# Last mixer: one product per head and level for both token tiles, a turned square at the end, and the exponent differences on GpSimd

## The chip, the cores and the metric

The kernel runs on one core of a Trainium2 chip. The time is device microseconds of that core, as the median of several runs; a profiled execution is one further run, in which every instruction's start and end were recorded. Its engines are called PE (TensorE, with PEld for its weight loads), DVE (VectorE), ACT (ScalarE), POOL (GpSimd) and SP (SyncE, which here issues the weight loads).

## What is computed

The reference is a chain of eight stages over 256 tokens of width 1024: a SwiGLU layer, an attention and gated linear attention mixer, a second SwiGLU layer, an embedding gate, a second mixer, a convolutional feed-forward layer, the HGRN2 mixer, and a last feed-forward layer. The change touches the HGRN2 mixer, the stage "hg". Cut to what matters:

```python
def hgrn2_chunkwise(q, k, v, log_f):
    # S_t = diag(f_t) S_{t-1} + k_t v_t^T with k_t = 1 - f_t, o_t = S_t^T q_t
    diff = G_[..., :, None, :] - G_[..., None, :, :]      # G: running sum of log_f
    pair_decay = jnp.exp(jnp.where(incl, diff, -jnp.inf))
    attn = jnp.einsum("bhld,bhlsd,bhsd->bhls", q_, pair_decay, k_)
    ...
def hgrn2_mixer(u, w_in, lower_bound, norm_gain, w_out):
    q, f, i, gate = jnp.split(u @ w_in, ...)
    log_f = jnp.logaddexp(jnp.log(lb), jnp.log1p(-lb) + jax.nn.log_sigmoid(ff))
    k = (1.0 - lb) * jax.nn.sigmoid(-ff)
    o = hgrn2_chunkwise(silu(q), k, i, log_f)             # 8 heads of 128
    y = head_rms_norm(o, norm_gain) * jax.nn.silu(gate)
    return y.astype(u.dtype) @ w_out
```

For every head the weight of key token j in query token i is the sum over 128 channels of q[i] * exp(G[i] - G[j]) * k[j], for j up to i.

## The kernel before

**Levels.** The kernel doesn't form the decay of each pair. It splits the triangle j < i into levels: at level `half` (128, 64, ..., 1: `ALL_LEVELS`, numbered n = 0 to 7) the tokens are cut in blocks of 2 x half, and the pairs with j in the left and i in the right half of one block are handled. With the value of G at the block's middle as a reference, the exponents G[i] - ref and ref - G[j] are computed apart (`dve_level_x`, two subtractions of 512 columns, lines 1695 and 1697), made into exponentials by ACT (`act_level`, line 1714), and multiplied into the queries and the keys by DVE (`dve_level_l`, lines 1707 and 1709). The result, `h_l[n % 2]`, has decayed keys in left and decayed queries in right places, 4 heads x 256 tokens wide. PE multiplies it with itself (`pe_h_level`, line 2394 by `per_tile`): one 128 x 128 product for each head and each of the two tiles of 128 tokens, 8 for a level, into one of two pairs of PSUM banks. DVE puts the part that belongs to the level into the square of attention weights, `h_at[u]`, by a copy under a mask (`dve_h_put`, line 2981; the masks are the constants `level64` to `level1`). Level 0 (half = 128) joins the two tiles, has 4 products (line 2956) and its own place `h_cross`; number 8 is the diagonal. All of these products are fp32, and an fp32 product of PE stands in the trace as two instructions.

**Units and steps.** The 8 heads are two units u of 4 heads. `H_STEPS` is the list of 18 steps g, nine for each unit in the order 8, 0, 1, ..., 7. m = 0 to 15 counts levels without the diagonal. Behind each step's products PE multiplies one or two half-slots ("pieces") of the projection weights (`pieces_after(g)`), which supply the forget gate, query, output gate and value of the units. Each fp32 weight piece is split into a high part by ACT (`split_hi`, line 298) and a low part by DVE (`split_lo`, line 303), each 1024 columns; PE multiplies three times with them (lines 329 to 331).

**Order.** The order on each engine is the order of the code, and every engine works through its queue strictly, waiting where an instruction waits. DVE's turn for one level m is: put of two steps back, the two products of level m, at times a scan of G for unit 1 (line 2900), the two differences of level m + 2, the low half of a weight piece. ACT's turn is: the high half of a piece, the exponential of level m + 2, and in some turns a block of its own: `act_h_forget(1)` at m = 2 (two sigmoids, a table load before and behind, four logarithms), `act_h_q(1)` at m = 5, the gates at m = 7 and 13. POOL in this stage has only two clearings of `h_at`.

**The end of the stage.** When a unit's squares are complete PE multiplies them with the values (`pe_h_out`, lines 3008 and 3010). ACT squares the output, DVE applies the gain and sums the squares, ACT takes the root, DVE gates (line 3044), PE turns the rows (line 337), ACT and DVE split them into high and low, and PE multiplies them with the output weights, pieces 0 to 7 of "hgo". For unit 1 the order on PE is: piece 0, output products of unit 1, pieces 1 and 2, turns of unit 1's rows, pieces 3 to 7.

Of the kernel before, what the change touches and what calls it, by code (L numbers as in the profile page):

```python
# [8 lines left out]
U32 = mybir.dt.uint32  # L9
# [30 lines left out]
def shape_constants():  # L40
# [11 lines left out]
    for name, f in (("cos", np.cos), ("sin", np.sin), ("nsin", lambda a: -np.sin(a))):  # L52
        for t in range(NT):
            parts[f"{name}{t}"] = f(ang[t].astype(np.float64))
    at, cols, n = {}, [], 0
    for name, a in parts.items():
        at[name] = n
        n += a.shape[1]
        cols.append(a.astype(np.float32))
# [30 lines left out]
def build(nc, A, out, numbered, stop=None):  # L90
# [3 lines left out]
    with ctx:  # L94
# [19 lines left out]
        const = sb("const", [P, A["const"].shape[1]])  # L114
# [57 lines left out]
        out_sem = sem("stored")  # L172

# [1514 lines left out]
        def dve_level_x(dve, X, n, half, b, e, ready):  # L1688
# [3 lines left out]
            for name in ready:  # L1692
                dve.wait_ge(*after(name))
            ref = blocks(b)[:, :, half - 1:half].broadcast_to([P, b.shape[1] // (2 * half), half])
            nc.vector.tensor_tensor(blocks(e)[:, :, right], blocks(b)[:, :, right], ref, ALU.subtract)\
                .then_inc(*steps.did("dve", f"{X}.x{n}r"))
            nc.vector.tensor_tensor(blocks(e)[:, :, left], ref, blocks(b)[:, :, left], ALU.subtract)\
                .then_inc(*steps.did("dve", f"{X}.x{n}"))
# [80 lines left out]
        def dve_g_exponents(dve, n):  # L1779

            dve_level_x(dve, "g", n, ALL_LEVELS[n], gb, g_e[n % 2], [f"g.l{n - 2}"] if n >= 2 else ["g.b"])
# [5 lines left out]
        def dve_g_levels(dve):  # L1787

            levels = len(ALL_LEVELS)
            for n in range(2, levels):  # L1790
                dve_g_put(dve, n - 1)
                dve_g_decayed(dve, n)
                if n + 2 < levels:
                    dve_g_exponents(dve, n + 2)
# [144 lines left out]
        def dve_mix0(dve):  # L1939
# [24 lines left out]
            dve_g_exponents(dve, 0)  # L1964
            dve_a_den(dve)
            dve_g_exponents(dve, 1)
# [3 lines left out]
            for n in range(2):  # L1970
                dve_g_decayed(dve, n)
                dve_g_exponents(dve, n + 2)
# [860 lines left out]
        h_sil = (arena[:, 10752:11776], hk[0])  # L2833
        h_sq = (hk[0], arena[:, 6144:7168])
# [103 lines left out]
        def pe_h_level(pe, g):  # L2938
# [15 lines left out]
            if n == 0:  # L2954
# [6 lines left out]
        def dve_h_put(dve, g):  # L2961
# [9 lines left out]
            before = {8: f"{X}.at0", 1: f"{X}.put8"}.get(n, f"{X}.put{n - 1}")  # L2971
            dve.wait_ge(*after(before))
            half = ALL_LEVELS[n] if n < len(ALL_LEVELS) else 0
            if half:
                right = lambda a: a.rearrange("p (k m r) -> p k m r", k=8, r=2 * half)[:, :, :, half:]
                mask = cst(f"level{half}").rearrange("p (m r) -> p m r", r=2 * half)[:, :, half:]
                mask = mask.bitcast(U32).unsqueeze(1).broadcast_to([P, 8, P // (2 * half), half])
            else:
# [404 lines left out]
```

## Time and profile before

| | us |
|---|---|
| median of 3 runs | 1234.22 |
| lowest, highest | 1234.01, 1234.27 |
| span of the profiled execution | 1232.7 |
| PE busy | 1215.1 |
| DVE busy | 847.2 |
| ACT busy | 682.4 |
| POOL busy | 53.0 |

The span is from the first to the last instruction; the median stands 1.5 us above it. The stage hg lies at about 885 to 1037 us. In a row of the order of time the time of an instruction runs from its start to its end; on a busy queue the next one starts a little before the end, so that the distance of the starts is the smaller number. "Idle before" is the time that the engine stood in front of it, with what ended it. The durations of PE's products overlap, and a sum of them says nothing; the union of their spans does.

### The profile page before, as it was taken

To read this page: it belongs to the slowest core of one execution; us is meant where nothing else is said; L and a number is where in the kernel's file an instruction comes from. 1 tells how busy PE (TensorE), PEld (TensorE's weight loads), DVE (VectorE), ACT (ScalarE), POOL (GpSimd) and SP (SyncE) were. 2 spreads that over 40 slices of the span, in tenths; PEclk is the share of its full clock that TensorE was granted. 3 is DMA by queue.
4 is the path that set the end of the run, shared out by engine and by line. 5 is a ranking of instruction groups with operands and counts; after the bars stand their busy time and mean duration, and the time that the engine had idled before them with its cause. 6 is when DMAs were issued, how large, how long until landed. Compare 5 with 4: busy or idle time off the path is not lost. (4 is left out here: it accounts for less than half of the span.)

```text
span 1232.7 us, 19105 instructions
## 1 busy us (share of the span) xinstructions
PE 1215.1 (99%) x7351; PEld 1069.0 (87%) x7351; DVE 847.2 (69%) x1153; ACT 682.4 (55%) x1009; POOL 53.0 (4%) x84
## 2 busy tenths in 40 slices
PE   8999999999999999999999999999999999999998
PEld 6888888887888888889898799999899887999997
DVE  5555457778654446757966776776868988766666
ACT  5444446464544435656635765555775657655455
POOL 0400000010000000101400000000000000000000
PEclk9999999999999999999999999999999999999999
DMA  9965555425645555544322665555553335555620
GB/s 336 272 221 175 174 205 175 138 69 171 212 173 174 183 204 205 174 157 138 134 69 87 205 205 192 176 172 177 204 205 100 107 100 209 178 185 184 204 103 35
DMA packets 139206, 209.10 MB, mean 170 GB/s; under 512 B 9949, under 2 KB 101235, under 8 KB 139137
## 3 DMA queue, kind: packets, MB, share of 16 engines
q1 hardware_dynamic: 136256, 199.39, 48.1%
q0 software_dynamic: 2864, 8.76, 2.5%
q8 instruction: 46, 0.75, 0.3%
q14 instruction: 24, 0.19, 0.0%
q10 hardware_dynamic: 16, 0.00, 0.0%
HBM read 207.08 MB, written 1.05 MB: 169 GB/s over the span
## 5 line engine op out<-in xcount | busy, mean ns | idle before, releaser
L303 DVE TENSOR_TENSOR wlo<-raw,whi 128x1024 fp32r<-128x1024 f32 x374 | 440.6, 1221 | 45.1 <-ACT whi L298 43.3
L298 ACT ACTIVATE whi<-raw 128x1024 fp32r<-128x1024 f32 x374 | 374.1, 1050 | 42.4 <-PE psum L331 40.4
L329 PE MATMUL psum<-whi,xh 128*128 128x512 f32 (+1 forms) x688 | 275.3, 400 | 4.8 <-DVE wlo L303 3.5
L331 PE MATMUL psum<-whi,xl 128*128 128x512 f32 (+1 forms) x688 | 267.4, 389 | 0.0
L330 PE MATMUL psum<-wlo,xh 128*128 128x512 f32 (+1 forms) x688 | 266.8, 388 | 0.0
L329 PE MATMUL psum<-xh,whi 128*128 128x256 f32 x928 | 263.5, 284 | 0.0
L330 PE MATMUL psum<-xl,whi 128*128 128x256 f32 x928 | 262.6, 283 | 0.0
L331 PE MATMUL psum<-xh,wlo 128*128 128x256 f32 x928 | 262.6, 283 | 0.0
L329 PEld LDWEIGHTS psum<-xh,whi 128*128 128x128 f32 x928 | 177.9, 192 | 0.9
L330 PEld LDWEIGHTS psum<-xl,whi 128*128 128x128 f32 x928 | 178.0, 192 | 0.7
L331 PEld LDWEIGHTS psum<-xh,wlo 128*128 128x128 f32 x928 | 178.0, 192 | 0.0
L329 PEld LDWEIGHTS psum<-whi,xh 128*128 128x128 f32 x688 | 129.6, 188 | 36.2 <-DVE wlo L303 4.2
L331 PEld LDWEIGHTS psum<-whi,xl 128*128 128x128 f32 x688 | 129.5, 188 | 27.5
L330 PEld LDWEIGHTS psum<-wlo,xh 128*128 128x128 f32 x688 | 129.8, 189 | 23.6
L329 PE MATMUL psum<-whi,hidh 128*128 128x512 f32 x352 | 137.5, 391 | 0.0
L330 PE MATMUL psum<-wlo,hidh 128*128 128x512 f32 x352 | 137.2, 390 | 0.0
L331 PE MATMUL psum<-whi,hidl 128*128 128x512 f32 x352 | 137.0, 389 | 0.0
L1175 DVE SCALAR_TENSOR_TENSOR arena<-psum,taps,arena 128x254 f32<-128x254 f32 (+1 forms) x176 | 74.8, 477 | 82.3 <-ACT arena L1141 78.1
L1195 DVE TENSOR_TENSOR hidl<-psum,hidh 128x512 fp32r<-128x512 f32 x22 | 15.2, 692 | 149.0 <-ACT hidh L1191 149.0
L1191 ACT ACTIVATE hidh<-psum 128x512 fp32r<-128x512 f32 x22 | 13.2, 598 | 166.0 <-PE psum L1076 166.0
L1141 ACT ACTIVATE arena<-psum,taps 128x256 f32<-128x256 f32 x88 | 42.4, 563 | 90.6 <-PE psum L331 79.8
L331 PEld LDWEIGHTS psum<-whi,hidl 128*128 128x128 f32 x352 | 66.1, 188 | 13.9
(373 smaller groups left out, 1184.5 us busy)
## 6 DMA issues: line engine op xcount, KB each, us to landing
raw<-in_ffn_w_up SPq DMA_DIRECT2D x131, 512.0 KB, 5.2
raw<-in_ffn_w_down SPq DMA_DIRECT2D x88, 512.0 KB, 4.4
raw<-in_ffn_w_gate SPq DMA_DIRECT2D x43, 512.0 KB, 4.6
raw<-in_c_w_in SPq DMA_DIRECT2D x32, 512.0 KB, 4.7
raw<-in_ab_w_in SPq DMA_DIRECT2D x28, 512.0 KB, 4.7
raw<-in_w_in SPq DMA_DIRECT2D x18, 512.0 KB, 4.5
raw<-in_w_out SPq DMA_DIRECT2D x8, 512.0 KB, 4.1
raw<-in_ple_w_gate SPq DMA_DIRECT2D x8, 512.0 KB, 5.0
```

Of the source, the lines that this page charges most:

```text
L298: nc.scalar.activation(hi, r, ACT.Copy).then_inc(hi_done, 1)
L303: nc.vector.tensor_tensor(lo, r, hi.bitcast(F32), ALU.subtract).then_inc(lo_done, 1)
L329: nc.tensor.matmul(pe_out, sh, mh, start=start, stop=False, skip_group_check=True)
L330: nc.tensor.matmul(pe_out, sh, ml, start=False, stop=False, skip_group_check=True)
L331: return nc.tensor.matmul(pe_out, sl, mh, start=False, stop=stop, skip_group_check=True)
L1141: last = nc.scalar.activation(cg[:, q, j, c, :], gate_or_up(n, q, j, c), ACT.Identity, scale=tap(n, 2, f), bias=tap(n, 3, f))
L1175: last = nc.vector.scalar_tensor_tensor(y, gate_or_up(n, q, j, c)[:, 0:SEQ - lag], tap(n, k, g * 2 + (FC * j + c)), y, ALU.mult, ALU.add)
L1191: nc.scalar.activation(hidh[:, q], hidden_columns(q) if n < 2 else hp[:, q], ACT.Copy).then_inc(hid_hi, 1)
L1195: nc.vector.tensor_tensor(hidl[:, q], hidden_columns(q) if n < 2 else hp[:, q], hidh[:, q].bitcast(F32), ALU.subtract)\
```

## The change

**One product for both tiles.** In levels 1 to 7 DVE now writes the decayed queries of tile 0 into the right places of tile 1 and the other way round (two products of 256 columns in place of one of 512; the keys as before). PE then multiplies, for each head, tile 0's part of `h_l` with tile 1's: left places of tile 0 are tile 0's keys and meet tile 0's queries, above the diagonal; right places of tile 0 are tile 1's queries and meet tile 1's keys, below the diagonal. So there are 4 products in place of 8 at these levels, and one square holds both tiles.

**Gathering.** The square of a unit is `h_both[u]`, 4 heads x 128. Level 1 is copied whole by ACT, level 2 by ACT in its two diagonal quarters (`act_h_put`, at m % 8 = 3 and 4), levels 3 to 7 by DVE under the masks `block32` to `block2`, new constants, 4 heads x 128 columns. `h_both[0]` lies where the masks `level64` to `level8` were; the new masks come by a DMA of POOL in the stage ffn2. Then DVE copies the upper triangle into tile 0 of `h_at[u]`, PE turns the square (4 transposes of 128 x 128, `pe_h_turn`), and DVE copies the upper triangle of the turned one into tile 1 (`dve_h_upper`).

**Order.** Unit 0's turn is behind step 9 and its output products move from step 9 to step 10. In the tail PE's order becomes: piece 0, turn of unit 1's square, piece 1, output products of unit 1, piece 2, turns of unit 1's rows, piece 3. On DVE both copies of unit 1's upper triangle stand ahead of the low halves of output pieces 1 to 3.

**Differences on GpSimd.** The exponent differences of m = 2 to 15 are issued by POOL, in order, with the same waits; those of m = 0 and 1 stay on DVE.

The diff, cut to its core:

```diff
+    late = {f"block{n}": (j // n == i // n) for n in (32, 16, 8, 4, 2)}
+    late["strict"] = (j < i)
...
+        h_both = (const[:, const_at["level1"]:const_at["level1"] + BANK], h_at[0][:, 0:BANK])
...
-            if n == 0:
+            if n < len(ALL_LEVELS):
                 for x in range(4):
                     last = nc.tensor.matmul(bank(b, x * P, P), head_tok(l)(0, x), head_tok(r)(1, x), start=True, stop=True)
...
+            mask = cst(f"block{2 * ALL_LEVELS[n]}").bitcast(U32).unsqueeze(1).broadcast_to([P, 4, P])
+            nc.vector.copy_predicated(by_head(h_both[u]), mask, by_head(bank(b))).then_inc(*steps.did("dve", f"{X}.put{n}"))
...
+        def act_h_put(act, u, n):
+
+            X = f"h{u}"
+            src, dst = by_head(bank(LEVEL_BANK[(9 * u + 1 + n) % 2])), by_head(h_both[u])
+            act.wait_ge(*after(f"{X}.P{n}"))
+            if n == 1:
+                if u == 1:
+                    act.wait_ge(*after("h0.O"))
+                nc.scalar.activation(dst, src, ACT.Copy).then_inc(*steps.did("act", f"{X}.put1"))
+                return
+            act.wait_ge(*after(f"{X}.put1"))
+            for p in halves:
+                last = nc.scalar.activation(dst[p, :, p], src[p, :, p], ACT.Copy)
+            last.then_inc(*steps.did("act", f"{X}.put2"))
+
+        TURNED_BANK = (1, 5)
+
+        def pe_h_turn(pe, u):
+
+            pe.wait_ge(*after(f"h{u}.put7"))
+            for x in range(4):
+                last = nc.tensor.transpose(bank(TURNED_BANK[u], x * P, P), h_both[u][:, x * P:x * P + P], ident)
+            last.then_inc(*steps.did("pe", f"h{u}.turned"))
+
+        def dve_h_upper(dve, u, t):
+
+            X = f"h{u}"
+            dve.wait_ge(*after(f"{X}.turned" if t else f"{X}.put7"))
+            dve.wait_ge(*after(f"{X}.put8"))
+            mask = cst("strict").bitcast(U32).unsqueeze(1).broadcast_to([P, 4, P])
+            src = bank(TURNED_BANK[u]) if t else h_both[u]
+            nc.vector.copy_predicated(by_head(h_at[u][:, t * BANK:t * BANK + BANK]), mask, by_head(src))\
+                .then_inc(*steps.did("dve", f"{X}.upper{t}"))
...
+            tiles = lambda a: a.rearrange("p (x t m r) -> p x t m r", x=4, t=2, r=2 * half)
+            for t in range(NT):
+                nc.vector.tensor_tensor(tiles(l)[:, :, 1 - t, :, half:], tiles(q)[:, :, t, :, half:], tiles(e)[:, :, t, :, half:], ALU.mult)\
+                    .then_inc(*steps.did("dve", f"h{u}.l{n}r{t}"))
+            blocks = lambda a: a.rearrange("p (m r) -> p m r", r=2 * half)[:, :, 0:half]
+            nc.vector.tensor_tensor(blocks(l), blocks(k), blocks(e), ALU.mult).then_inc(*steps.did("dve", f"h{u}.l{n}"))
...
                 if g == 9:
+                    pe_h_turn(pe, 0)
+                if g == 10:
                     pe_h_out(pe, 0)
...
+            pe_h_turn(pe, 1)
+            pe_out(pe, "hgo", 1)
             pe_h_out(pe, 1)
-            for k in (1, 2):
-                pe_out(pe, "hgo", k)
+            pe_out(pe, "hgo", 2)
...
+                if m % 8 in (3, 4):
+                    act_h_put(act, m // 8, m % 8 - 2)
...
-                    if k >= 0:
+                    if k >= 0 and H_STEPS[k][1] not in (1, 2):
                         dve_h_put(dve, k)
+                if m == 8:
+                    dve_h_upper(dve, 0, 0)
                 dve_h_decayed(dve, m)
+                if m == 8:
+                    dve_h_upper(dve, 0, 1)
                 if m == 3:
                     dve_h_key(dve, 1)
                 if 3 <= m < 7:
                     dve_h_decay(dve, 1, m - 3)
-                if m + 2 < 16:
-                    dve_h_exponents(dve, m + 2)
                 for k in (g + 1, g + 2) if m == 7 else (g + 1,):
                     for p in pieces_after(k):
...
             dve_h_put(dve, 17)
+            dve_h_upper(dve, 1, 0)
+            dve_h_upper(dve, 1, 1)
             out_splits(split_lo, dve, "hgo", (1, 2, 3))
...
             nc.gpsimd.memset(h_at[0], 0.0).then_inc(*steps.did("pool", "h0.at0"))
+            for m in range(2, 10):
+                h_exponents(pool, nc.gpsimd, "pool", m)
             pool.wait_ge(*after("h0.l7"))
             pool.wait_ge(*after("h0.P8"))
             nc.gpsimd.memset(h_at[1], 0.0).then_inc(*steps.did("pool", "h1.at0"))
+            for m in range(10, 16):
+                h_exponents(pool, nc.gpsimd, "pool", m)
             next_gain(pool, gains)
```

DVE in unit 0, from the low halves of two weight pieces to the products of level 3, before. The numbers are the shape of the output; in brackets stand the semaphores that the instruction waits for.

```order
L303 TENSOR_TENSOR wlo<-raw,whi 128x1024 [waits hi_done] x2
L2969 COPY arena<-psum 128x512 [waits pe_done]
L1707 TENSOR_TENSOR arena<-arena 128x16x32 [waits act_done,pe_done]
L1709 TENSOR_TENSOR arena<-arena 128x16x32
L1695 TENSOR_TENSOR arena<-arena 128x64x8 [waits dve_done]
L1697 TENSOR_TENSOR arena<-arena 128x64x8
L303 TENSOR_TENSOR wlo<-raw,whi 128x1024 [waits hi_done]
L2981 COPY_PREDICATED arena<-const,psum 128x8x64 [waits dve_done,pe_done]
L1707 TENSOR_TENSOR arena<-arena 128x32x16 [waits act_done,pe_done]
L1709 TENSOR_TENSOR arena<-arena 128x32x16
```

And now, over the same levels:

```order
L310 TENSOR_TENSOR wlo<-raw,whi 128x1024 [waits hi_done] x2
L2977 COPY arena<-psum 128x512 [waits pe_done]
L3047 TENSOR_TENSOR arena<-arena 128x4x2x32 [waits act_done,pe_done]
L3047 TENSOR_TENSOR arena<-arena 128x4x2x32
L3050 TENSOR_TENSOR arena<-arena 128x16x32
L310 TENSOR_TENSOR wlo<-raw,whi 128x1024 [waits hi_done]
L3047 TENSOR_TENSOR arena<-arena 128x4x4x16 [waits act_done,pe_done]
L3047 TENSOR_TENSOR arena<-arena 128x4x4x16
L3050 TENSOR_TENSOR arena<-arena 128x32x16
```

The differences (lines 1695 and 1697) are gone, and so is the put of level 1; the product of the queries stands twice (line 3047). The first masked put of unit 0 comes two levels later than before.

ACT, around the forget gate of unit 1: before.

```order
L1714 ACTIVATE arena<-arena 128x1024 [waits dve_done]
L2876 ACT_TABLE_LOAD
L2876 ACTIVATE arena<-psum 128x1024 [waits used]
L2877 ACTIVATE arena<-psum 128x1024
L388 ACT_TABLE_LOAD
L2885 ACTIVATE arena<-arena,small 128x256 [waits act_done,dve_done]
L2885 ACTIVATE arena<-arena,small 128x256 x3
L298 ACTIVATE whi<-raw 128x1024 [waits used,loaded3]
L1714 ACTIVATE arena<-arena 128x1024 [waits dve_done]
```

And now:

```order
L1721 ACTIVATE arena<-arena 128x1024 [waits pool_done]
L2884 ACT_TABLE_LOAD
L2884 ACTIVATE arena<-psum 128x1024 [waits used]
L2885 ACTIVATE arena<-psum 128x1024
L395 ACT_TABLE_LOAD
L2893 ACTIVATE arena<-arena,small 128x256 [waits act_done,dve_done]
L2893 ACTIVATE arena<-arena,small 128x256 x3
L2999 ACTIVATE const<-psum 128x512 [waits pe_done]
L305 ACTIVATE whi<-raw 128x1024 [waits used,loaded3]
L1721 ACTIVATE arena<-arena 128x1024 [waits pool_done]
L3003 ACTIVATE const<-psum 64x4x64 [waits act_done,pe_done]
L3003 ACTIVATE const<-psum 64x4x64
```

The exponential (1714, now 1721) waits for POOL in place of DVE, and the copies of levels 1 and 2 (lines 2999 and 3003) stand behind the block of the forget gate.

DVE in the tail of the stage, from the last put of unit 1: before.

```order
L2981 COPY_PREDICATED arena<-const,psum 128x256x2 [waits dve_done,pe_done]
L352 TENSOR_TENSOR xl<-psum,xh 128x4x128 [waits act_done] x2
L2981 COPY_PREDICATED arena<-const,psum 128x512 [waits dve_done,pe_done]
L303 TENSOR_TENSOR wlo<-raw,whi 128x1024 [waits hi_done] x3
L3034 TENSOR_TENSOR arena<-psum,gain 128x2x512 [waits act_done,gain_in1]
L3027 TENSOR_REDUCE small<-arena 128x8 [waits act_done]
L3044 SCALAR_TENSOR_TENSOR arena<-arena,small 128x128 [waits act_done,dve_done]
```

And now:

```order
L2986 COPY_PREDICATED arena<-const,psum 128x512 [waits late_masks_in,dve_done,pe_done]
L359 TENSOR_TENSOR xl<-psum,xh 128x4x128 [waits act_done] x2
L2986 COPY_PREDICATED arena<-const,psum 128x512 [waits late_masks_in,dve_done,pe_done]
L3022 COPY_PREDICATED arena<-const,arena 128x512 [waits dve_done]
L3022 COPY_PREDICATED arena<-const,psum 128x512 [waits dve_done,pe_done]
L310 TENSOR_TENSOR wlo<-raw,whi 128x1024 [waits hi_done] x3
L3086 TENSOR_TENSOR arena<-psum,gain 128x2x512 [waits act_done,gain_in1]
```

Two copies of the upper triangle (line 3022), of which the second waits for PE's turn, stand ahead of the low halves of output pieces 1 to 3.

## Rows read from the trace of the kernel before

**Rows 1.** The page's first part: busy us (share of the span) and instructions.

```profile
PE 1215.1 (99%) x7351; PEld 1069.0 (87%) x7351; DVE 847.2 (69%) x1153; ACT 682.4 (55%) x1009; POOL 53.0 (4%) x84
```

**Rows 2.** Stretches of ten us: length, busy us of each engine, granted clock, DMA.

```profile
10.00:20.00 10.00, 9.66 (x40) 7.61 (x40) 6.18 (x8) 7.73 (x20) 0.00 (x0) 0.85 1.08 363
980.00:990.00 10.00, 10.00 (x66) 9.00 (x66) 9.73 (x14) 5.99 (x8) 0.00 (x0) 1.00 0.27 99
```

**Rows 3.** Groups of 880 to 1030: shapes, count, busy us, mean ns, idle.

```profile
L303 DVE TENSOR_TENSOR wlo<-raw,whi 128x1024 fp32r<-128x1024 f32 x40 | 47.8, 1222 | 7.7 <-ACT whi L298 7.5
...
L2394 PE MATMUL psum<-arena 128*128 128x128 f32 x256 | 31.1, 275 | 0.0
...
L2981 DVE COPY_PREDICATED arena<-const,psum 128x512 f32<-128x512 uint32 x14 | 12.5, 891 | 1.7 <-PE psum L2394 1.5
L1695 DVE TENSOR_TENSOR arena<-arena 128x512 f32<-128x512 f32 x16 | 11.0, 687 | 1.6 <-DVE arena L2900 0.2
L1709 DVE TENSOR_TENSOR arena<-arena 128x512 f32<-128x512 f32 x16 | 11.0, 686 | 0.0
...
L347 ACT ACTIVATE xh<-psum 128x512 fp32r<-128x512 f32 x8 | 4.5, 594 | 2.4 <-PE psum L337 2.3
```

**Rows 4.** Order of time, PE: start us, us, engine, line, tiles, count, idle.

```profile
988.58 1.95 PE L2394 MATMUL psum<-arena 128*128 128x128 f32 x16
...
993.12 1.95 PE L2394 MATMUL psum<-arena 128*128 128x128 f32 x16
...
1012.73 1.28 PE L3008 MATMUL psum<-arena 128*128 128x128 f32 x10
...
1020.95 0.66 PE L337 MATMUL psum<-const,arena 128*128 128x128 f32 x4
```

**Rows 5.** Order of time, DVE, one turn of unit 0.

```profile
952.82 0.68 DVE L2900 TENSOR_TENSOR_SCAN arena<-small,arena 128x256 f32<-128x256 f32 x1
953.42 0.67 DVE L1695 TENSOR_TENSOR arena<-arena 128x512 f32<-128x512 f32 x1
...
954.60 1.22 DVE L303 TENSOR_TENSOR wlo<-raw,whi 128x1024 fp32r<-128x1024 f32 x1
955.74 0.70 DVE L2981 COPY_PREDICATED arena<-const,psum 128x512 f32<-128x512 uint32 x1
...
956.93 0.69 DVE L1709 TENSOR_TENSOR arena<-arena 128x512 f32<-128x512 f32 x1
```

**Rows 6.** Groups of POOL over the whole program.

```profile
L2375 POOL TENSOR_TENSOR arena<-arena,gain 128x1024 f32<-128x1024 f32 x2 | 4.7, 2362 | 33.8 <-ACT arena L2732 33.7
...
L1423 POOL TENSOR_TENSOR arena<-const,small 128x64 f32<-128x64 f32 x8 | 2.3, 317 | 6.6 <-DMA small<-in_gla_w_gate_up 6.6
```

**Rows 7.** Order of time, DVE and POOL at 586 us, POOL's select; all splits.

```profile
586.55 2.49 DVE L303 TENSOR_TENSOR wlo<-raw,whi 128x1024 fp32r<-128x1024 f32 x2 [3.50 <-ACT whi L298]
...
586.74 2.48 POOL L2430 TENSOR_TENSOR arena<-const 128x64 f32<-128x64 f32 x2 [20.73 <-PE psum L2304]
...
563.11 0.63 POOL L2247 TENSOR_SCALAR_AFFINE_SELECT arena<-arena 128x512 f32<-128x512 f32 x1
...
L303 DVE TENSOR_TENSOR wlo<-raw,whi x374: 1203/1220/1345, 8.4 to 1217.9; 128x1024 fp32r<-128x1024 f32 x187
```

**Rows 8.** Order of time, ACT, blocks of the forget gate and the query.

```profile
936.42 1.06 ACT L1714 ACTIVATE arena<-arena 128x1024 f32<-128x1024 f32 x1 [3.49 <-DVE arena L1697]
...
944.03 1.04 ACT L298 ACTIVATE whi<-raw 128x1024 fp32r<-128x1024 f32 x1
...
955.79 1.28 ACT L2905 ACT_TABLE_LOAD   x1
...
959.42 1.06 ACT L298 ACTIVATE whi<-raw 128x1024 fp32r<-128x1024 f32 x1
```

**Rows 9.** Order of time, DVE's gates and PE's second turn in the tail.

```profile
1019.76 2.19 DVE L3044 SCALAR_TENSOR_TENSOR arena<-arena,small 128x128 f32<-128x128 f32 x8 [0.67 <-DVE small L3027]
...
1022.00 0.66 PE L337 MATMUL psum<-const,arena 128*128 128x128 f32 x4 [0.40 <-DVE arena L3044]
```

More of the change, by code:

```diff
@@ L58, in shape_constants @@
         n += a.shape[1]
+        cols.append(a.astype(np.float32))
+    at["late"] = n
+    for m, (name, a) in enumerate(late.items()):
+        at[name] = at["level64"] + m * P
         cols.append(a.astype(np.float32))
@@ L2970, in dve_h_put @@
                 return
[L2971 to L2978, printed above, removed]
-                right = lambda a: a.rearrange("p (k n) -> p k n", k=8)
-                mask = ident.bitcast(U32).unsqueeze(1).broadcast_to([P, 8, P])
@@ L2981, in dve_h_put @@
-            nc.vector.copy_predicated(right(h_at[u]), mask, right(wide2(b))).then_inc(*steps.did("dve", f"{X}.put{n}"))
-        def dve_h_exponents(dve, m):
+            dve.wait_ge(*after(f"{X}.at0" if n == 8 else f"{X}.put{n - 1}"))
+            if n == 8:
+                mask = ident.bitcast(U32).unsqueeze(1).broadcast_to([P, 8, P])
+                nc.vector.copy_predicated(eight(h_at[u]), mask, eight(wide2(b))).then_inc(*steps.did("dve", f"{X}.put8"))
+                return
+            dve.wait_ge(late_masks_in, 16)
@@ L3002, in pe_h_out @@
             b = O_BANK[u]
-            for r in (f"{X}.put7", f"{X}.put0", f"hv{u}") + (("hgo.xl10",) if u == 1 else ("hs0",)):
+            for r in (f"{X}.upper0", f"{X}.upper1", f"{X}.put0", f"hv{u}") + (("hgo.xl10",) if u == 1 else ("hs0",)):
                 pe.wait_ge(*after(r))
@@ L3172, in dve_hg, with pool_late_masks @@
             first_pieces(split_lo, dve, "ffn3", (0, 1))
+        def pool_late_masks(pool):
+            for name in ("dXT.m", "d.masks"):
+                pool.wait_ge(*after(name))
+            late = A["const"][:, const_at["late"]:]
+            pool.dma_start(const[:, const_at["level64"]:const_at["level64"] + late.shape[1]], late).then_inc(late_masks_in, 16)
         def pool_hg(pool, gains):
             nc.gpsimd.memset(h_at[0], 0.0).then_inc(*steps.did("pool", "h0.at0"))
+            for m in range(2, 10):
+                h_exponents(pool, nc.gpsimd, "pool", m)
             pool.wait_ge(*after("h0.l7"))
@@ L3196, in pool_params @@
         def pool_params(pool):
-            loads = [(const[:, P:], A["const"][:, P:])]
+            loads = [(const[:, P:], A["const"][:, P:const_at["late"]])]
             for l in range(2):
```

47 lines of the change are left out of this document (29 added, 18 removed).

## Prediction

> **What bounds the kernel now.** Read the busy times first: PE is busy 1215.1 of 1232.7 us, DVE 847.2 [rows 1]. The stretches of ten us then show where the change lies, the last mixer (about 885 to 1037 us): PE is busy 10.00 of 10.00 and DVE 9.73 at 980 to 990 [rows 2]. So two engines are full there, and a saving on PE is worth something only if DVE, and what DVE waits for, keep up. The groups of the stretch give prices [rows 3], the order of time gives the beat: from one level's products to the next 4.54 us (988.58 to 993.12), 1.80 for the level's products and 2.74 for one piece of projection [rows 4]. DVE's turn for one level [rows 5]: a scan 0.60 (four turns only), the exponent differences 2 x 0.60, the low half of a weight piece 1.14, the put 0.60, the two products of the decayed keys and queries 1.20, so 4.74 us, or 4.14 without the scan.
>
> All prices below are times from one start to the next on a busy queue, from these rows. With them I kept a ledger of the four queues from 922.9 us on, each instruction beginning at the later of its queue's turn and what it waits for. Kept for the order of before, it puts the level at 988.6, unit 1's output products at 1012.6 and the turns of its gated rows at 1020.7; the rows have 988.58, 1012.73 and 1020.95 [rows 4]. The same ledger for the new order gives the waits named below.
>
> **PE's own work.** A level's 8 products are 16 instructions in 1.95 us, of which the last one's 0.27 overlaps what follows [rows 3, 4]: 0.112 us an instruction, 0.225 a product. 14 levels (64 to 1 of two units) lose 4 products: 56 x 0.225 = -12.6 us. Added: 8 turns of the squares at about 0.11, +0.9 (four take 0.66 with the last one's tail [rows 4]). Net **-11.7 us**, if nothing else moves.
>
> **DVE's own work.** 28 of the 32 differences leave: -28 x 0.60 = -16.8. Four puts leave for ACT, -2.4. The puts of halves 2 and 1 cost more today: 14 puts take 12.5 us, the ordinary one 0.70 [rows 3, 5], so the four fine ones about 1.35 each. With whole rows of 128 I take 0.62 to the next, -2.5 together; if the fine puts stayed dear it would cost DVE that much and the path about half. Four copies of the upper triangle: +2.5. The queries' product cut in two of 256 columns: 0.33 each, +0.06 x 14. Without GpSimd in its way, DVE's turn would be 2.9 to 3.5 us, under PE's new 3.64 (0.90 + 2.74).
>
> **What GpSimd costs.** No row has this instruction at 512 columns. At 1024 a two-input one takes 2.36 us, at 64 it takes 0.317 [rows 6]: 0.18 + 2.13 ns a column, so 1.27 alone and 1.24 in a row. 28 of these is 35 us, where DVE spent 17. Bounds: 1.09 (the columns alone) and 1.45 (short runs of 1, 2 and 4 columns costing some of their own); below lies 0.63, the one-input select of 512 columns [rows 7], which I take only for the rival.
>
> The more important row is what it does beside DVE. Two 64-column instructions of GpSimd, 0.32 alone, took 2.48 us for the two, one beside each of two DVE splits running from 586.55 [rows 7]. Each ended just after a split. And the longest split of all 374 is 1.345 us against a median of 1.220 [rows 7]: the two of 586.55 take 2.49 where 1.14 + 1.22 = 2.36 would do, so the second was held about 0.13 us, as long as GpSimd's 64 columns take. So when both read two operands of SBUF, one waits for the other, in turns. The Trainium skill, page SBUF — State Buffer, section Who interferes with whom, says the same of a DVE instruction with two SBUF inputs against a GpSimd one that reads SBUF, and has the port held for the whole instruction, where the rows fit a hold of the columns only; by the rule the ledger would end 3.8 us later than by the rows (1249.8 in place of 1246.0). It also exempts DVE instructions with one SBUF input; no row here has such a pair at 512 columns, and the sum would be the same, since I let the put (mask and PSUM) pass anyway.
>
> One turn in the new order with these holds, unit 0, from the end of level 4's products: scan 0.6; the split then waits for the first difference, 1.0; split 1.14; put 0.6, while the second difference, which had waited for the split, runs; the queries' product waits 0.4 for its end; products 1.3. That is 5.0 us in place of 4.74, and 4.5 in place of 4.14 without the scan: **DVE's turn does not get shorter**, and PE, needing 3.64, waits 0.9 to 1.4 in each such turn.
>
> **The sum on PE, wait by wait (ledger at 1.24).** Level 5 and 6 of unit 0: 1.1 + 1.4, as just worked out. Level 3 of unit 0: 3.6. ACT copies level 1 (0.59, by ACT's 512 columns [rows 3]) only behind the forget gate of unit 1, a block that today runs with the exponential before it from 936.42 to 944.03 [rows 8]; that exponential now waits for GpSimd until 939.5, the copy ends at 947.5, and PE has been ready since 943.9. Level 7 of unit 0: 4.0. After an exponential ACT loads a table, does silu and loads the table back, and only then splits: 955.79 to 959.42 today [rows 8], covered by PE's 4.54 a level; in the new order DVE gets that split 4.0 late and level 7 is queued behind it. Unit 1: 0.3 + 1.5 + 1.5 + 1.6 at levels 8, 2, 3, 4 (the square of unit 0's output is one step later, and ACT's splits queue behind it; then the turns). The turns of unit 0's rows wait 2.2 for ACT's gate, which is behind the last exponential. First output piece: 2.1, was 0.4.
>
> Then the tail, where the code's order alone makes the wait. DVE stands at the turned square before it splits output pieces 1 to 3, so PE waits turn, copy and split: 0.15 + 0.6 + 1.2 = 2.1. And between unit 1's output products and the turns of its gated rows lies one output piece of 2.74 instead of two. The chain it has to cover is square, gain, sums, root and gates, from 1015.3 to the gates that began at 1019.76; today two pieces cover it to within 0.40 [rows 9]. One piece less leaves 2.6 + 0.5.
>
> Sum of waits 24.5, against 1.0 in the same places today: +23.5. With -11.7: **+11.8 us**. The profiled run would be 1232.7 + 11.8 = 1244.5; the median stands 1.5 above that span, so **1246.0 us**. Behind 1037 us PE is busy throughout and nothing gives time back. The loads of this stage are the same ones, further apart: nothing. The 0.4 MB of late masks go in while ffn2 runs, behind no one: nothing. GpSimd's next gain is queued behind its last difference, as it was behind the memset, and waits for a later step anyway.
>
> **Rivals.** (1) GpSimd is held by DVE but DVE is not held by GpSimd (the 0.13 us is chance). The ledger gives +4.6: 1238.8. For it: only one long split shows the other direction. (2) No contention at all at 512 columns: +1.7, 1235.9. What remains is ACT's order and the tail. Against it: the held splits [rows 7]. (3) The other side, **faster**: the differences run at the rate of the select, 0.63 us, and do not contend. Then the ledger gives -3.2, 1231.0; it is break-even at about 1.0 us an instruction and reaches -2.5 at 0.7. The tail's 4.7 us stay even then, so -11.7 is out of reach. For it: PE's saving is certain and DVE is relieved. Against: both two-input sizes [rows 6]. (4) Slower still: runs of 1, 2 and 4 columns double GpSimd's time, as fine masks double DVE's puts (8 to 12 instructions x 1.1), or PE's clock falls in the idle stretches of 4 us; the one place with such idleness, the opening, had 0.85 granted after it [rows 2], 1.5 us in ten. Either gives +16 to +20, 1250 to 1254. That the change does not do what it says is excluded: the products and the moved differences stand in the instruction order.
>
> **Chances.** Forecast with its own range 1242 to 1250: 0.57. (1) 0.14, (2) 0.10, (3) 0.12, (4) 0.07. A measurement of this kernel can tell 0.2%, 2.5 us. Faster by that: (3), 0.12. Within: (2) and a little of its neighbours, 0.11. Slower: 0.77. The range leaves out (3) and the far end of (4): 1234.5 to 1254.
>
> **What will show it.** In the stage: PE busy well under 10 of 10, about 24 us of waits before level products 3 and 7 of unit 0, levels 2 to 4 of unit 1 and in the tail; GpSimd's differences at 1.24 us where DVE is idle and 2.2 to 2.4 where they meet a split; DVE's splits and products often at their time plus 1.0. The prediction is wrong if splits stay at 1.22 beside a running difference (then 1), if the differences are at 1.27 throughout (then 2), or well below one us (then 3). The step from unit 1's output products to the turns should be one piece plus 3 us in every case.

## The result: 1249.07 us, and the profile after

The changed kernel takes 1249.07 us in the median (1246.79 to 1250.64), the kernel before 1234.24. The ratio is 1.0114, 95% interval 1.0099 to 1.0129: 12 to 16 us slower (14.8 by the medians), where 12 were forecast. One of the four runs of the kernel before, 1492.5 us, was a slow one and is left out of the ratio. The profiled execution of the changed kernel is one of its two longer ones (1250.57 us), with a span of 1248.6 us, 15.9 more than before. The four executions had 1250.6, 1247.6, 1246.8 and 1250.6 us at a mean granted clock of 0.991, 0.993, 0.995 and 0.991, the two longer ones at the lower clock. The busy times of the profiled one, against [rows 1]:

```profile
PE 1212.7 (97%) x7247; PEld 1062.7 (85%) x7247; DVE 840.1 (67%) x1139; ACT 684.7 (55%) x1015; POOL 93.2 (7%) x113
```

PE has 104 instructions fewer and DVE 14 fewer, and PE's share of the span fell. The stretches of 20 us (length, busy us of PE, PEld, DVE, ACT, POOL, granted clock, DMA share, GB/s) show where. TensorE's granted clock is given as a share of 2.4 GHz:

```profile
940.00:960.00 20.00, 16.14 (x111) 14.32 (x110) 13.95 (x22) 13.99 (x18) 8.44 (x6) 1.00 0.24 86
960.00:980.00 20.00, 16.17 (x84) 13.90 (x83) 13.30 (x17) 13.29 (x13) 8.88 (x7) 0.83 0.30 106
980.00:1000.00 20.00, 16.50 (x93) 13.54 (x92) 14.89 (x19) 10.47 (x14) 7.74 (x7) 1.00 0.24 74
1000.00:1020.00 20.00, 16.64 (x86) 13.89 (x86) 16.13 (x27) 11.49 (x12) 5.01 (x4) 0.92 0.25 85
1020.00:1040.00 20.00, 15.04 (x69) 11.99 (x69) 11.77 (x18) 6.35 (x9) 0.58 (x1) 0.84 0.41 131
```

PE has gaps in every stretch, and neither DVE nor any other engine is full: the engines wait for each other in a ring. PE's waits from 900 to 1060 us (line waiting, line waited for, total, times, longest):

```profile
PE psum L2964 <- DVE arena L3050: 7.7, 5, 3.8
PE psum L344 <- DVE arena L3096: 3.0, 2, 2.6
PE psum L2964 <- ACT const L2999: 2.6, 1, 2.6
PE psum L336 <- DVE xl L359: 2.2, 1, 2.2
PE psum L336 <- DVE wlo L310: 1.9, 1, 1.9
PE psum L344 <- ACT arena L2930: 1.2, 1, 1.2
PE psum L2964 <- ACT arena L2999: 0.9, 1, 0.9
```

That is 19.5 us in 12 places, against 0.9 in 3 places over the same stretch before. (L2964 are the level products of one square, L336 the first product of a weight piece, L344 the turns of the gated rows, L3050 the product of the decayed keys, L2999 ACT's copy of a level, L3096 the gates, L359 and L310 low halves, L2930 a gate on ACT.) The two longest waits of unit 0 in PE's order of time are those before levels 3 and 7:

```profile
946.56 1.16 PE L2964 MATMUL psum<-arena 128*128 128x128 f32 x8 [2.57 <-ACT const L2999]
...
967.12 2.04 PE L2964 MATMUL psum<-arena 128*128 128x128 f32 x8 [3.83 <-DVE arena L3050]
968.82 0.77 PE L336 MATMUL psum<-whi,xh 128*128 128x512 f32 x1
969.39 0.63 PE L337 MATMUL psum<-wlo,xh 128*128 128x512 f32 x1
969.82 0.63 PE L338 MATMUL psum<-whi,xl 128*128 128x512 f32 x1
```

Behind the second of them stands what the forecast had left to a rival. The eight products take 2.04 us where such eight take 1.05 elsewhere, and the 512-column products behind them begin 0.43 us after one another instead of 0.23. PE's granted clock is 0.50 from 966 to 972 us, the lower of its two levels (1.2 GHz), where before it has 2.4 GHz throughout the stage. That is the 0.83 of the second row above. It fell again in the tail (0.92 and 0.84 in the last two rows), where before every row has 1.00.

GpSimd beside DVE, one turn of unit 0 in both orders of time:

```profile
950.50 2.00 DVE L310 TENSOR_TENSOR wlo<-raw,whi 128x1024 fp32r<-128x1024 f32 x1
952.42 0.74 DVE L2986 COPY_PREDICATED const<-const,psum 128x512 f32<-128x512 uint32 x1
953.05 0.96 DVE L3047 TENSOR_TENSOR arena<-arena 128x256 f32<-128x256 f32 x2
953.93 0.68 DVE L3050 TENSOR_TENSOR arena<-arena 128x512 f32<-128x512 f32 x1
954.53 0.68 DVE L2908 TENSOR_TENSOR_SCAN arena<-small,arena 128x256 f32<-128x256 f32 x1
```

```profile
950.15 1.26 POOL L1702 TENSOR_TENSOR arena<-arena 128x512 f32<-128x512 f32 x1 [8.20 <-DVE arena L3050]
951.38 2.02 POOL L1704 TENSOR_TENSOR arena<-arena 128x512 f32<-128x512 f32 x1
...
960.11 1.05 POOL L1702 TENSOR_TENSOR arena<-arena 128x512 f32<-128x512 f32 x1 [2.08 <-DVE arena L2908]
961.12 1.04 POOL L1704 TENSOR_TENSOR arena<-arena 128x512 f32<-128x512 f32 x1
```

At 960 us DVE is idle, and the two differences take 1.05 and 1.04 us. At 950 us the split issued at 950.50 stands until the first difference is over, then runs its 1.2 us; the second difference stands until the split is over, and takes 2.02. The put, whose second operand is PSUM, has 0.74 beside a running difference. From scan to scan the turn takes 4.63 us (949.90 to 954.53), where before it took 4.74 with the two differences in it.

### The profile page after: what moved, and what is told of

Its sections match the earlier page's. It is cut to its first block and busy times, and to the rows that moved or that the text cites. A ratio compares the mean times of both kernels' runs of the same rounds, so it can differ in the third digit from the quotient of the medians.

```text
span 1248.6 us, 18922 instructions
## 1 busy us (share of the span) xinstructions
PE 1212.7 (97%) x7247; PEld 1062.7 (85%) x7247; DVE 840.1 (67%) x1139; ACT 684.7 (55%) x1015; POOL 93.2 (7%) x113
## 3 DMA queue, kind: packets, MB, share of 16 engines
HBM read 207.47 MB, written 1.05 MB: 167 GB/s over the span
## 5 line engine op out<-in xcount | busy, mean ns | idle before, releaser
L310 DVE TENSOR_TENSOR wlo<-raw,whi 128x1024 fp32r<-128x1024 f32 x374 | 444.9, 1231 | 58.3 <-ACT whi L305 56.6
L336 PE MATMUL psum<-whi,xh 128*128 128x512 f32 (+1 forms) x688 | 277.8, 404 | 8.2 <-DVE wlo L310 5.1
L336 PE MATMUL psum<-xh,whi 128*128 128x256 f32 x928 | 263.5, 284 | 0.0
L336 PEld LDWEIGHTS psum<-xh,whi 128*128 128x128 f32 x928 | 177.9, 192 | 1.0
L336 PEld LDWEIGHTS psum<-whi,xh 128*128 128x128 f32 x688 | 131.1, 191 | 39.8 <-DVE wlo L310 5.6
L336 PE MATMUL psum<-whi,hidh 128*128 128x512 f32 x352 | 137.5, 391 | 0.0
L338 PEld LDWEIGHTS psum<-whi,hidl 128*128 128x128 f32 x352 | 66.1, 188 | 13.8
```

The lines of the kernel that those rows point to most:

```text
L310: nc.vector.tensor_tensor(lo, r, hi.bitcast(F32), ALU.subtract).then_inc(lo_done, 1)
L336: nc.tensor.matmul(pe_out, sh, mh, start=start, stop=False, skip_group_check=True)
L338: return nc.tensor.matmul(pe_out, sl, mh, start=False, stop=stop, skip_group_check=True)
```

## The experiments

The opening of the program differs from execution to execution (PE is busy for 32.4 to 36.4 of its first 40 us), and a mixer that is the same up to there begins up to 4.2 us later, which is noise on a span. So beside the times stands the **stage's length**: from the start of the first level product to the start of PE's second turn of unit 1's rows (924.97 and 1022.00 us before, 97.0 us). Two profiles of one kernel agree in it within 0.03 us (e2 and e10, e8 and e11). "Waits" are PE's idle times from 940 to 1056 us, added up from its order of time; 0.2 us of them lie behind the stage's end in some kernels. "Clock" is the time lost by the granted clock, (1 - clock) x 20 us over the stretches from 940 to 1060; in idle time it costs nothing, so it is a bound. Stage, waits and clock are of one profiled execution each. The ratios are against runs of the kernel before from the same session, whose medians went from 1234.17 to 1235.72.

| kernel | median us | ratio, 95% | stage us | waits | clock |
|---|---|---|---|---|---|
| before | 1234.24 | | 97.0 | 0.9 | 0 |
| after | 1249.07 | 1.0099-1.0129 | 111.9 | 19.5 | 8.6 |
| e1, differences on DVE | 1241.37 | 1.0037-1.0070 | 102.7 | 14.2 | 3.6 |
| e3, GpSimd only writes | 1239.08 | 1.0022-1.0044 | 100.9 | 12.0 | 3.6 |
| e2, e10, before + GpSimd | 1241.91, 1239.56 | 1.0032-1.0065, 1.0030-1.0058 | 101.6, 101.6 | 3.9 | 1.8 |
| e4, idle places filled | 1244.87 | 1.0068-1.0105 | 106.4 | 5.1 | 0 |
| e5, output products first | 1243.99 | 1.0054-1.0090 | 104.7 | 13.8 | 5.4 |
| e6, ACT's order | 1241.00 | 1.0031-1.0068 | 102.0 | 13.7 | 3.6 |
| e7, both orders | 1235.61 | 0.9999-1.0023 | 97.5 | 11.1 | 0 |
| e8, e11, both, DVE | 1231.41, 1232.26 | 0.9967-0.9988, 0.9963-0.9984 | 94.1, 94.0 | 7.7 | 0 |
| e9, both, alternating | 1232.08 | 0.9967-0.9991 | 94.1 | 8.1 | 0 |

### What GpSimd's share costs: e1, e3, e2

**e1** is the change with all exponent differences on DVE:

```diff
+        ON_POOL = ()
...
                     dve_h_decay(dve, 1, m - 3)
+                if m + 2 < 16 and m + 2 not in ON_POOL:
+                    h_exponents(dve, nc.vector, "dve", m + 2)
...
-                h_exponents(pool, nc.gpsimd, "pool", m)
+                if m in ON_POOL:
+                    h_exponents(pool, nc.gpsimd, "pool", m)
```

> The changed kernel with the exponent differences of levels m = 2 to 15 back on DVE, everything else as changed. Theory (GpSimd and DVE hold each other; ACT's order, the tail and a lower clock of PE do the rest): the holds go, DVE has 16.8 us more work of its own. The ledger gives +3.8 us against the kernel before, and the clock still falls where PE stands idle in the tail, 2 to 4 us more: 1239 to 1243. Rival A (the loss lies in the order on ACT and in the tail and in the clock alone, GpSimd costs nothing): as the changed kernel, 1247 to 1250.

It took 1241.37 us, 7.7 less than with GpSimd. The longest split is 1.346 us again (2.145 in the changed kernel). DVE's turn is 4.82 us from scan to scan (947.88 to 952.70), so that moving two of its differences to GpSimd had shortened it by 0.2 us only.

**e3** leaves GpSimd where it is, but lets it write zeros in place of the differences, without reading anything: twice over all 1024 columns, where each difference writes 512 of them. The level weights are then wrong; the instructions of the other engines stay.

```diff
+            if who == "pool":
+                api.memset(e, 0.0).then_inc(*steps.did(who, f"{X}.x{n}r"))
+                eng.wait_ge(*after(f"{X}.x{n}r"))
+                api.memset(e, 0.0).then_inc(*steps.did(who, f"{X}.x{n}"))
+                return
```

> The changed kernel, in which GpSimd writes zeros over the exponent buffer twice (0.95 us each, with a wait between) in place of computing the two differences, so it reads nothing; the attention weights of levels 16 and lower and of unit 1 are then wrong. Same queue, same waits, about the same time on GpSimd. Theory (the holds need both engines to read SBUF): splits at 1.22 us beside GpSimd, the ledger gives -0.4 to +0.8 plus 3 to 5 for the clock: 1237 to 1240. Rival C (what costs is the longer way over GpSimd, not the holding; or any GpSimd instruction holds DVE): 1246 to 1250, splits up to 2.1 us in the second case.

It took 1239.08 us. The same turn, on both engines:

```profile
947.30 1.20 DVE L310 TENSOR_TENSOR wlo<-raw,whi 128x1024 fp32r<-128x1024 f32 x1
948.41 0.74 DVE L2991 COPY_PREDICATED const<-const,psum 128x512 f32<-128x512 uint32 x1
949.04 0.75 DVE L3052 TENSOR_TENSOR arena<-arena 128x256 f32<-128x256 f32 x2
949.70 0.69 DVE L3055 TENSOR_TENSOR arena<-arena 128x512 f32<-128x512 f32 x1
950.30 0.69 DVE L2913 TENSOR_TENSOR_SCAN arena<-small,arena 128x256 f32<-128x256 f32 x1
```

```profile
946.92 0.95 POOL L1703 MEMSET arena<- 128x1024 f32 x1 [9.32 <-DVE arena L3055]
947.93 0.95 POOL L1705 MEMSET arena<- 128x1024 f32 x1
```

The writes take nearly as long as the differences (0.95 and 1.05), overlap the same split, and neither engine is held: the split has 1.20, and scan to scan (946.70 to 950.30) is 3.60 instead of 4.63 us. So it is the reads that hold. Against the changed kernel the stage is 11.0 us shorter, of which 7.5 are waits; most of the rest fits the clock, whose bound falls from 8.6 to 3.6.

The finding agrees with the Trainium skill, page SBUF — State Buffer, section Who interferes with whom: a DVE instruction with two SBUF inputs contends with a GpSimd one that reads SBUF, not with one that only writes it. The same page, section SBUF: two separate sides, has the one that starts first hold the port for its whole instruction. That is met within about 0.15 us here: the products of 953.05 take 0.96 us beside a difference that goes on until 953.40, and 0.75 alone, so they are held for 0.21 of those 0.35 us.

**e2** is the other half: the kernel before, all 8 products a level kept, with only the differences moved to GpSimd.

```diff
-                if m + 2 < 16:
-                    dve_h_exponents(dve, m + 2)
...
+            for m in range(2, 10):
+                dve_h_exponents(pool, m, nc.gpsimd, "pool")
```

> The kernel before with only one part of the change: the differences of m = 2 to 15 on GpSimd. Theory: DVE is held while a difference runs, GpSimd takes 1.05 us alone (as the trace of the changed kernel shows) and 2.0 behind a split; the ledger gives +2.8 us, 1236 to 1239, and DVE's splits show times up to 2.1 us. Rival B (no holding, DVE is simply relieved of 16.8 us): 1234 within 0.5, since PE was busy throughout anyway, and splits at 1.22.

It took 1241.91 us, above what either side expected, so it was run once more:

> Edit: none against the kernel before with the differences alone on GpSimd; it is the same kernel once more, since in its first profile the last mixer began 4.2 us later than in the kernel before, in which nothing of the edit lies. Theory (the 4.2 us are the opening's, they come and go from run to run, and the edit itself costs what lies behind its first product): the mixer's first product on VectorE begins within 1 us of 922.9, and the time is 1238 to 1241. Rival (the edit costs 7 us by itself): the mixer begins at 922 to 924 and the time is 1241 to 1243 all the same.

The first level product began at 929.20 us in the first profile and at 925.94 in the second (924.97 before), and the stage took 101.6 us in both. So the edit costs 4.6 us in the stage, in both profiles, and the first profile's other 4.2 lie ahead of it. The first median stays a miss: 1236 to 1239 was expected. The second, 1239.56, is in the range given for it. Of the 4.6 us the waits are 2.9, which is the ledger's +2.8, and the clock behind them, which the ledger does not have, is the rest:

```profile
971.20 3.55 PE L2395 MATMUL psum<-arena 128*128 128x128 f32 x16 [2.96 <-DVE arena L1710]
```

Sixteen instructions take 3.55 us instead of 1.95 [rows 4]: 1.6 us for a wait of 3. The wait comes by way of ACT: the exponential ahead of the query's block with its table loads waits for GpSimd and starts at 958.96 in e10, 954.72 before, which is 3.3 us later counted from the stage's start, and the next split stands behind that block.

### What the clock costs: e4

**e4** gives PE products with zeros in its idle places, so that it is seldom idle; they accumulate zero or go into a bank that is free.

```diff
+        FILL_AT = {4: 8, 6: 1, 7: 2, 8: 12, 12: 4, 13: 3, 14: 5}
...
+            if g in FILL_AT:
+                pe_fill(pe, FILL_AT[g], 1, True)
```

> The changed kernel with products of zeros on PE (0.23 us each, 1 to 12 in a row, into a bank nobody reads or as an added zero) in the places where PE stands idle, always fewer than the idle time there. Theory (the clock falls behind idle stretches and costs the 6 to 7 us that the ledger at 1.05 us a difference does not explain): granted clock 1.00 in all stretches, 1241 to 1244. Rival D (the lower clock only fills time in which PE would wait anyway): 1248 to 1251, as the changed kernel or a little slower.

More work, less time: 1244.87 us, 4.2 less than the change, and 5.5 us off the stage. That is 0.9 above the theory's range and far from the rival's 1248 to 1251. Two of the same stretches as above:

```profile
960.00:980.00 20.00, 18.95 (x116) 16.35 (x115) 13.31 (x18) 13.58 (x14) 8.88 (x7) 1.00 0.33 107
...
1020.00:1040.00 20.00, 19.13 (x98) 15.34 (x97) 14.69 (x21) 10.68 (x15) 0.58 (x1) 1.00 0.61 198
```

The clock stays at 2.4 GHz, and nothing but PE's idle places was touched. The clock had thus cost at least 5.5 of the 14.9 us by which the stage grew in that profile.

### What the order of the code costs: e5, e6, e7

**e5** moves unit 1's output products ahead of output piece 1, on PE alone:

```diff
             pe_h_turn(pe, 1)
-            pe_out(pe, "hgo", 1)
             pe_h_out(pe, 1)
-            pe_out(pe, "hgo", 2)
+            for k in (1, 2):
+                pe_out(pe, "hgo", k)
```

> Edit: on TensorE alone, the two output products of unit 1's rows go ahead of the first piece of the output projection (after the change they stand behind it and wait there for the square's turn); no other engine's order changes. Theory (each place costs the wait that its row shows, and the wait of 1.92 us at the output piece and that of 2.64 us at the last turn overlap with the moved work): 3.9 us less than the changed kernel, 1243.5 to 1246.5, and the wait of 2.6 us for the gates L3096 falls under 0.5. Rival (the gates' chain on VectorE sets the end whatever TensorE does before it): within 1 us of the changed kernel, 1248 to 1250, with a wait of the same size left in front of the last turn.

1243.99 us, 5.1 less. The wait of 2.64 us for the gates is gone, and 0.40 is left before the second turn, as before the change; of the changed kernel and of e5:

```profile
1035.87 0.66 PE L344 MATMUL psum<-const,arena 128*128 128x128 f32 x4 [2.64 <-DVE arena L3096]
```

```profile
1019.97 1.35 PE L3060 MATMUL psum<-arena 128*128 128x128 f32 x10 [0.86 <-DVE arena L3022]
...
1028.26 0.65 PE L344 MATMUL psum<-const,arena 128*128 128x128 f32 x4
1029.32 0.66 PE L344 MATMUL psum<-const,arena 128*128 128x128 f32 x4 [0.40 <-DVE arena L3096]
```

**e6** changes the order on ACT, and one place on DVE:

```diff
                 if m == 2:
+                    act_h_put(act, 0, 1)
+                if m in (2, 5, 8):
+                    for p in pieces_after(step_of(m + 1) + 1):
+                        split_hi(act, p)
+                if m == 13:
+                    out_splits(split_hi, act, "hgo", (0,))
+                if m == 2:
                     act_h_forget(act, 1)
```

Each of these is taken out of the later place where it stood, so that it now runs ahead of the block with the table loads or the gate; DVE's split for step 4 goes ahead of its work on unit 1's keys, where it waited behind it.

> Edit: ScalarE's copy of level 1 goes ahead of the forget block's table work, the high halves of the next weights go ahead of the exponential at steps 2, 5 and 8 and of the output gate at step 13, and VectorE's low halves for step 4 go ahead of its products at step 3. Nothing is added or removed. Theory (the waits at products 3, 5, 6 and 7 of unit 0 are ScalarE's and VectorE's order, not the sum of their work): the four waits of 2.57, 0.52, 0.77 and 3.83 us fall under 3 us together, TensorE's clock does not fall between 960 and 980, and the time is 5 us less than that of the changed kernel, 1242 to 1245.5. Rival (the products on VectorE, held by GpSimd's differences, set the pace there): the waits only change their names, and the time is 1247 to 1250.

1241.00 us, 8.1 less, where 5 were expected; it is 1 us below the range. The four waits named are 2.4 us together: the 2.57 before level 3 are gone and the 3.83 before level 7 are 1.16. Two new ones come, 1.39 at level 4, for the copy of level 2, and 1.09 at unit 1's first products. The clock has 1.00 up to 1000 us.

**e7** has both:

> Edit: the two edits of the output products' place and of ScalarE's order together, with GpSimd's differences as the change has them. Theory (the two terms add, and with fewer idle places the clock's part goes too): the sum of durations gives 1.6 us less than the kernel before where no slow clock is left; with 0 to 5 us of it left, 1232.5 to 1239. Rival (the differences on GpSimd hold VectorE and set a floor of their own): above 1241, near 1243.

1235.61 us, within 0.2% of the kernel before, and the clock is at 1.00 in every stretch of the profile (1235.82 us; four of the twelve runs took 1238 to 1240, at 0.996 or 0.997). But 11.1 us of waits in 12 places remain, and the stage is 0.5 us longer than before, where the sum of durations had it 1.6 shorter.

### The same products without GpSimd's reads in the way: e8, e9

**e8** is e7 with all differences on DVE (the edit of e1); **e9** has every second product's on GpSimd (`ON_POOL = (3, 5, 7, 9, 11, 13)`).

> Edit: as the kernel with both edits of order, and all exponent differences on VectorE, so that GpSimd has none. Theory (the change's saving of 56 products on TensorE, 12.6 us, is real and is lost only in waits at named places, of which this kernel removes most): the sum of durations gives 3.0 us less than the kernel before, 1231; with 0 to 4 us of slow clock left, 1230 to 1235. Rival (VectorE's 28 extra differences, 17 us, set the pace once the order is mended, so the two edits bring little over differences on VectorE alone at 1241.4): 1238 to 1242.

> Edit: as the kernel with both edits of order, but of the exponent differences those of every second product stay on GpSimd (products 3, 5, 7, 9, 11, 13) and the others are made on VectorE. Theory (GpSimd's differences take 8 us off VectorE and hold its splits only at half as many places): the sum of durations gives 3.3 us less than the kernel before, 1231, no better than all on VectorE by more than 0.5 us: 1230.5 to 1233.5. Rival (each meeting with a split costs the whole stretch, also when there are half as many): halfway between the two measured kernels, 1231.4 and 1235.6, or above: 1233.5 to 1236.

1231.41 and 1232.08 us: both beat the kernel before, by 0.23% (0.12 to 0.33) and 0.21% (0.09 to 0.33). In the stage, 3.0 us are gained in both. PE's waits in e9:

```profile
PE psum L2964 <- DVE arena L3051: 2.1, 2, 1.3
PE psum L2964 <- ACT arena L3003: 1.8, 1, 1.8
PE psum L2401 <- DVE const L2986: 1.1, 1, 1.1
PE psum L336 <- DVE xl L359: 0.9, 1, 0.9
PE psum L3061 <- DVE arena L3023: 0.9, 1, 0.9
PE psum L344 <- ACT arena L2930: 0.8, 1, 0.8
```

The profiled execution of e8 was its longest (1237.74), so it too was run again:

> Edit: none against the kernel with both edits of order and all differences on VectorE; the same kernel once more, since its first profile was one of its longest runs (1237.7 beside a median of 1231.4). Theory (the kernel is 2.8 us faster than the one before, and the long profile had its extra time outside the last mixer): the profiled span is 1229 to 1230.5, and TensorE's waits in the mixer are those of the first profile within 0.5 us each. Rival (the kernel has a cost that shows in some executions): a span over 1232 again, with other waits in the mixer.

The span was 1232.5, not the 1229 to 1230.5 expected; the stage has 94.0 us and the same eleven waits, so of the rival only the span came true. The ratio again is below 1 (0.9974). In both profiles the extra time lies ahead of the stage, whose first level product begins at 931.26 and 927.84, and one stretch far from any edit has a fallen clock (of e8, of e11):

```profile
640.00:680.00 40.00, 38.66 (x264) 34.47 (x264) 20.57 (x32) 17.60 (x30) 3.02 (x2) 0.87 0.23 77
640.00:680.00 40.00, 37.86 (x258) 33.13 (x258) 22.91 (x35) 17.37 (x30) 3.02 (x2) 0.91 0.22 67
```

The other eleven profiles have 1.00 there. The wait ahead of it is the same in all thirteen, 0.77 or 0.78 us:

```profile
656.08 0.66 PE L2486 MATMUL psum<-const,arena 128*128 128x128 f32 x4 [0.77 <-DVE arena L2550]
```

```profile
655.85 1.11 PE L2493 MATMUL psum<-const,arena 128*128 128x128 f32 x4 [0.77 <-DVE arena L2557]
```

The first is of the kernel before, the second of e11. That both profiles with the low clock are of one kernel may be chance: eight of e8's eleven runs and seven of e11's nine have a mean granted clock of 0.998 or more. Why this stage's clock falls in some executions was not tried.

## Why the prediction came out near, term by term

It said 1246.0 and the time was 1249.07. The main mechanism was right: PE's shorter work is lost in waits at named places. Three terms of the sum were mis-sized: the saving and the waits were put too large, and the clock was put at nothing. The last two nearly cancel.

- **PE's own work, -11.7.** Too large. Stage length less waits is 96.3 us before, and where the clock stayed up 86.6 (e7, e8) and 86.1 (e9): **-10**. The step that failed took one price, 0.225 us, for every product, and let a wait cost its idle time alone. Sixteen instructions are 1.70 us to the next start before (988.58 to 990.28). Eight are 0.81 in a full queue, but 0.88 behind a wait, and half of the levels now wait. And idle time is counted from the end of the last product, 0.39 us behind its start, where a full queue starts the next one after 0.23: each wait costs some 0.16 us more than it shows. For e7, with nine more waits in the stage than before and six waiting levels, an estimate from these rows is -11.7 + 9 x 0.16 + 6 x 0.07 = -9.9, where it has -9.7; for e9, with six and three, -10.5, where it has -10.1. The changed kernel's rows:

```profile
950.43 1.05 PE L2964 MATMUL psum<-arena 128*128 128x128 f32 x8
951.24 0.47 PE L336 MATMUL psum<-whi,xh 128*128 128x512 f32 x1
...
997.74 0.39 PE L337 MATMUL psum<-wlo,xh 128*128 128x512 f32 x1
997.97 0.39 PE L338 MATMUL psum<-whi,xl 128*128 128x512 f32 x1
999.78 1.13 PE L2964 MATMUL psum<-arena 128*128 128x128 f32 x8 [1.42 <-DVE arena L3050]
1000.66 0.47 PE L336 MATMUL psum<-whi,xh 128*128 128x512 f32 x1
```

- **The difference on GpSimd, 1.24 us.** Measured 1.05 us where nothing holds it, below even the lower bound of 1.09. The line through 64 and 1024 columns was the wrong ruler between them. With it DVE's turn was to be 5.0 us; it is 4.63.
- **The holding, both ways.** Right, though it had rested on one long split [rows 7]: splits take up to 2.15 us and differences beside them up to 2.04. e3 shows that it is the reading. Rivals (1) and (2) fall by these rows; so does (3), since 1.05 is not 0.63 and they contend.
- **The waits, 24.5 in all.** Measured 19.5, by the places forecast. Level 3 of unit 0: 3.6, was 2.57. Levels 5 and 6: 1.1 + 1.4, were 0.52 + 0.77. Level 7: 4.0, was 3.83. Unit 1's levels: 0.3 + 1.5 + 1.5 + 1.6, were 0, 1.14, 0.94, 1.42. Unit 0's turns 2.2, was 1.21. The tail, 2.1 + 2.1 + 2.6 + 0.5, was 2.15 + 1.92 + 2.64 + 0.40. Where GpSimd's price stands in a wait it was too long; where the code's order alone makes it, it was right to 0.2 us.
- **The clock, 0 in the forecast.** This is the largest error: up to 8.6 us by the granted clock, 5.5 at least by e4. The stage less its waits is 92.4 us after the change, against 86.1 to 86.6 with the clock up, which makes it some 6. It stood in rival (4) beside another cause, at 0.07 for the two, and so half of that rival came true inside the forecast's range. The row for it was there: [rows 2] had 0.85 behind idle time in the opening. A forecast of 24 us of waits in a stretch that had none should have carried a price for the clock in its main sum.

With the measured terms, +18.6 of waits, -10 of work and 5.5 to 8.6 of clock give +14.1 to +17.2; the stage grew by 14.9 and the span by 15.9. The waits were put 5 us too long, the saving 2 too large, and the clock, some 6, was missing: that the sum ended only 3 us off is partly luck.

The last sentence of the prediction held: from unit 1's output products to the turns one piece and 3 us. It held because of the order of the code, and e5 undid it by moving one call.

## What to carry to other kernels

When work leaves the engine that is full, write down what each other engine has queued between two of its handovers to it: here the saving of 10 us and 15 us more were lost, in good part to copies and weight splits that stood behind a table load or a gate, which earlier longer products had covered, and two reorderings brought 13.5 of 14.8 us back. Moving two-input work to GpSimd took next to nothing off a VectorE that spends its turn on two-input instructions (4.63 us a turn against 4.82 in e1), since the two take turns, and with the order mended it cost 3.5 us of the stage (e7 against e8). And add the clock to the price of any set of waits of some microseconds on TensorE; filling those places with idle products is a cheap experiment that gives a lower bound for its part of the loss.

## What the hardware showed that I had not expected

- A two-input fp32 instruction of GpSimd over 128 x 512 takes 1.04 to 1.07 us alone (2.36 for 1024 columns and 0.32 for 64 stand in [rows 6]); it is not on the line between them. One of its two operands is a repeated column; whether that makes it was not tried.
- Whether a wait of 2 to 4 us brings the clock down is no fixed thing: the same wait of 2.57 us before level 3 of unit 0 was followed by 2.4 GHz in the changed kernel (eight products in 1.16 us, above) and by 1.2 GHz in e5, which is the same program up to there. The wait of 0.77 us at 656 us shows the same (above, at e11). Waits of up to 2.17 us, 11.1 in all, left the clock at 1.00 in e7. In e5's order of time:

```profile
946.19 1.64 PE L2964 MATMUL psum<-arena 128*128 128x128 f32 x8 [2.57 <-ACT const L2999]
```

- The puts of halves 2 and 1 take 0.72 to 0.78 us each under masks of whole rows of 128 columns (two in 1.56 at 970.03, and 0.72 and 0.74 at 1014.73 and 1016.54), where the four fine ones before took some 1.35 each. Which part of the masks' form makes it was not tried.
